# Summing all eight conditioning panels on TensorE, a new order of the first RWKV products, and a place of its own for the third RWKV weight panel

## The reference

```python
c_act = silu(c)
ada = c_act @ ada_w + ada_b                       # (1024) x (1024, 6144)
shift1, scale1, gate1, shift2, scale2, gate2 = split(ada, 6)
h = rms_norm(x, norm_mix_w) * (1 + scale1) + shift1
u = h @ w_in
da_q, da_k, da_v, hg_f, hg_i, hg_q, hg_g, rw_u, gates = split(u)
o_a, o_b, o_c = diff_attention(...), hgrn2(...), rwkv7(rw_u, ...)
x = x + gate1 * (the three branches, gated, projected and merged)
h = rms_norm(x, norm_ffn_w) * (1 + scale2) + shift2
x = x + gate2 * swiglu(h)
out = rms_norm(x, final_norm_w)
# in rwkv7: u = u + (u_prev - u) * mu, u_prev being u one token earlier
```

## Time and profile before

| what | us |
|---|---|
| median of 3 runs (1193.88 to 1200.45) | 1193.95 |
| the profiled execution | 1193.82 |
| its span | 1192.0 |
| PE busy in the span | 1106.1 |
| DVE busy | 622.2 |
| ACT busy | 469.2 |

### The profile page before, as it was taken

How to read it: one execution, slowest core, us unless ns; L and a number is a source line. 1 busy time by engine, 2 the same in 40 slices (tenths; PEclk the granted TensorE clock), 3 DMA queues, 4 the chain that set the end, 5 groups by cost and what they waited for, 6 DMA issues and landing times.

```text
span 1192.0 us, 18345 instructions
## 1 busy us (share of the span) xinstructions
PE 1106.1 (93%) x7721; PEld 895.2 (75%) x7721; DVE 622.2 (52%) x858; ACT 469.2 (39%) x576; POOL 28.0 (2%) x49
## 2 busy tenths in 40 slices
PE   3999999889999998889998999998999999999995
PEld 2788757778887677778776777877888888878874
DVE  4487665364453256865855549744255343243244
ACT  6332542323232446665646665254222222223222
POOL 0100000000000000002000010000000000000000
PEclk9999989999999999999999999998999999999997
DMA  9767413311012531119521167412344422322301
GB/s 343 264 208 247 153 62 125 102 47 46 12 47 82 210 115 62 54 54 294 193 96 45 62 242 253 168 54 71 106 142 140 141 93 85 106 102 75 106 1 71
DMA packets 106202, 145.44 MB, mean 122 GB/s; under 512 B 3188, under 2 KB 86376, under 8 KB 106120
## 3 DMA queue, kind: packets, MB, share of 16 engines
q1 hardware_dynamic: 92392, 107.15, 27.2%
q0 software_dynamic: 6240, 23.48, 5.7%
q10 hardware_dynamic: 7488, 13.63, 3.1%
HBM read 128.53 MB, written 15.73 MB: 121 GB/s over the span
## 4 chain that ended last, share of the span: by engine, by line
PE 73%; DVE 12%; ACT 9%; issue 3%; DMA 2%; ACTq 0%; SPq 0%; POOL 0%; DVEq 0%
PE bank L2019 72%; DVE wlo L1340 2%; ACT whi L859 1%; DMA qk<-early_out 1%; DMA cond<-in_ada_w 1%; ACT gate_row L874 1%; ACT LX L1027 1%; DVE x L1340 1%; DVE Z L1340 1%; DVE SC L1340 0%; DVE mg L1340 0%; DVE f_tmp L1340 0%; DVE q_lev L1340 0%; DVE y L1343 0%; ACT L1261 0%
## 5 line engine op out<-in xcount | busy, mean ns | idle before, releaser
L2019 PE MATMUL bank<-hhi,whi 128*128 128x512 f32 (+1 forms) x832 | 336.4, 404 | 14.2 <-DVE hlo L1340 7.4
L2019 PE MATMUL bank<-hlo,whi 128*128 128x512 f32 (+1 forms) x832 | 326.2, 392 | 0.0
L2019 PE MATMUL bank<-hhi,wlo 128*128 128x512 f32 (+1 forms) x832 | 325.6, 391 | 0.0
L1340 DVE TENSOR_TENSOR wlo<-raw,whi 128x2048 fp32r<-128x2048 f32 (+1 forms) x80 | 170.6, 2132 | 262.5 <-ACT whi L859 261.6
L859 ACT ACTIVATE whi<-raw 128x2048 fp32r<-128x2048 f32 (+1 forms) x80 | 143.0, 1788 | 225.3 <-PE bank L2019 194.2
L2019 PEld LDWEIGHTS bank<-hhi,whi 128*128 128x128 f32 x832 | 160.4, 193 | 57.0 <-DVE hlo L1340 8.4
L2019 PEld LDWEIGHTS bank<-hhi,wlo 128*128 128x128 f32 x832 | 159.9, 192 | 33.5
L2019 PEld LDWEIGHTS bank<-hlo,whi 128*128 128x128 f32 x832 | 160.4, 193 | 30.7 <-issue 0.5
L2019 PE MATMUL bank<-whi,d_hi 128*128 128x512 f32 x160 | 63.3, 396 | 3.3 <-DVE d_lo L1340 3.3
L2019 PE MATMUL bank<-wlo,d_hi 128*128 128x512 f32 x160 | 63.1, 395 | 0.0
L2019 PE MATMUL bank<-whi,d_lo 128*128 128x512 f32 x160 | 63.1, 395 | 0.0
(11 more groups left out here) (343 smaller groups left out, 1555.1 us busy)
## 6 DMA issues: line engine op xcount, KB each, us to landing
raw<-in_w_in SPq DMA_DIRECT2D x33, 1024.0 KB, 5.4
raw<-in_f_in SPq DMA_DIRECT2D x22, 1024.0 KB, 5.0
raw<-in_ada_w SPq DMA_DIRECT2D x16, 1024.0 KB, 5.3
early_out<-gate_row ACTq DMA_DIRECT2D x52, 256.0 KB, 2.1
raw<-in_f_out SPq DMA_DIRECT2D x11, 1024.0 KB, 4.8
cond<-in_ada_w SPq DMA_DIRECT2D x8, 1024.0 KB, 10.8
sg<-early_out POOLq DMA_DIRECT2D x4, 1536.0 KB, 11.5
raw<-in_w_out SPq DMA_DIRECT2D x4, 1024.0 KB, 5.1
```

The lines of the kernel that those rows point to most:

```text
L1340: return v.tensor_tensor(out_, a, b, op)
L2019: return t.matmul(out_, lhsT, rhs, start=start, stop=stop, skip_group_check=True)
```

## The change

- The sums of all eight "first" panels are made on PE by one function (`row(f)` in place of `scale(q)`); ACT copies each result into its place of `ada_acc`. DVE's four `ada_sum` calls and `s_shift_sum` go. A shift section now takes 2 matmuls in `ada`, as a scale section did.
- DVE writes `x_norm`, not ACT.
- w2 (m = 2) gets a place of its own (`third_hi`, `third_lo`, where cond 4 and cond 5 lay), and is split in the head: by ACT ahead of `first_h(6)`, by DVE after `first_low(7)`. In the loop each of ACT and DVE is then one weight panel further on: step n takes panel m = n + 2 where it took m = n + 1, with the late sums behind that panel; step 1 first makes the sums behind w2.
- PE's hand-written order of the first products is another.

Cut to its core (declarations of semaphores left out, `at`, slot lists and the second norm's count too):

```diff
@@ panel_slots
-    slots = [2 if m == total - spare else 3 if m == total - 1 else (m + (m > total - spare)) % RING for m in range(total)]
+    own = {2: RING + 2, total - spare: RING, total - 1: RING + 1}
+    shared = [m for m in range(total) if m not in own]
+    slots = [own[m] if m in own else shared.index(m) % RING for m in range(total)]
@@ bank_plan
     for q in range(4):
-        b.add("scale", q)
+        b.add("row", 2 * q)
+        b.add("row", 2 * q + 1)
@@ build
+        third_hi = at("third_hi", 80, [P, 2048], F32R)
+        third_lo = at("third_lo", 88, [P, 2048], F32R)
@@ cond_released
-            if f % 2:
-                eng.wait_ge(*full("scale", f // 2))
-            else:
-                eng.wait_ge(s_shift_sum, f // 2 + 1)
+            eng.wait_ge(*full("row", f))
@@ gpsimd
-            pool.wait_ge(s_shift_sum, 4)
-            pool.wait_ge(*full("scale", 3))
+            pool.wait_ge(*full("row", 7))
@@ scalar
-            def scale_row(q):
+            def row(f):
+                act.wait_ge(*full("row", f))
+                if f >= 2:
+                    act.wait_ge(*full("ada", ADA[f - 2]))
+                do(ada_acc[:, f % 2, 0, :], bank_of("row", f)[:, 0:256], ACT.Copy).then_inc(free_sem("row", f), 1)
+                act.wait_ge(*freed("row", f))
...
-            for tb in range(TB):
-                norm_scaled(0, tb, x_in, x_norm)
-            scale_row(0)
+            row(0)
+            row(1)
             split_hi()
             first_h(0)
             first_h(1)
-            scale_row(1)
+            row(2)
+            row(3)
             split_hi()
             first_h(2)
             first_h(3)
-            for q in range(2, 4):
-                scale_row(q)
-                first_h(2 * q)
-                first_h(2 * q + 1)
+            row(4)
+            row(5)
+            first_h(4)
+            first_h(5)
+            row(6)
+            row(7)
+            split_hi()
+            first_h(6)
+            first_h(7)
 
             for n in range(7):
-                if n:
+                if 0 < n < 6:
                     split_hi()
@@ vector
+            def sums_behind(i):
                 while i + 1 < len(panels) and panels[i + 1][0] == "ada":
                     i += 1
                     late_sum(i)
+            def take_panel():
+                m = split_next[0]
+                if m < len(weights):
+                    take_low()
+                    sums_behind(weights[m])
...
             for tb in range(TB):
                 row_rstd(0, tb)
-            ada_sum(0, first_at[0])
+                ts(x_norm[:, tb, :], x_in[:, tb, :], col(RSTD + tb), ALU.mult).then_inc(s_x_normed, 1)
+                dve.wait_ge(s_x_normed, up(s_x_normed))
             conditioned(0)
             take_panel()
...
-            ada_sum(1, first_at[2])
             conditioned(1)
             take_panel()
...
-            ada_sum(2, first_at[4])
             conditioned(2)
-            ada_sum(3, first_at[6])
             first_low(4)
             first_low(5)
             conditioned(3)
...
             first_low(6)
             first_low(7)
+            take_low()
 
             for n in range(7):
-                if n:
+                if n == 1:
+                    sums_behind(weights[2])
+                if 0 < n < 6:
                     take_panel()
@@ tensor
             def ada(n):
-                if n < 4:
-                    pe.wait_ge(s_shift_sum, n + 1)
-                elif n < 8:
-                    pe.wait_ge(*freed("scale", n - 4))
+                if n < 8:
+                    pe.wait_ge(*freed("row", ADA.index(n)))
...
-                parts = 1 if 4 <= n < 8 else 2
+                parts = 1 if n < 8 else 2
...
-            scale(0)
+            row(0)
+            row(1)
             ada(0)
             ada(4)
             transposes((0, 1))
-            scale(1)
+            units = [[begin("rw", 2 * n + m) for m in range(2)] for n in range(2)]
+            row(2)
+            row(3)
             transposes((2, 3))
             ada(1)
             ada(5)
-            units = [[begin("rw", 2 * n + m) for m in range(2)] for n in range(2)]
             first = [next_panel()]
             unit_part(first[0], 0, units[0], (0, 1))
+            row(4)
             first.append(next_panel())
             unit_part(first[1], 1, units[1], (0, 1))
-            unit_part(first[0], 0, units[0], (2, 3))
-            scale(2)
+            row(5)
             transposes((4, 5))
             ada(2)
             ada(6)
+            unit_part(first[0], 0, units[0], (2, 3))
             unit_part(first[1], 1, units[1], (2, 3))
-            scale(3)
+            row(6)
+            row(7)
             transposes((6, 7))
             ada(3)
+            ada(7)
             unit_part(first[0], 0, units[0], (4, 5))
-            ada(7)
+            unit_part(first[1], 1, units[1], (4, 5))
             unit_part(first[0], 0, units[0], (6, 7))
-            unit_part(first[1], 1, units[1], (4, 5))
             unit_part(first[1], 1, units[1], (6, 7))
```

More of the change, by code:

```diff
@@ L516, in build @@
         s_cond_in = [sem(f"cond_in{f}") for f in range(8)]
-        s_shift_sum = sem("shift_sum")
         s_ca_wide = sem("ca_wide")
@@ L570, in build @@
         s_normed = sem("normed")
+        s_x_normed = sem("x_normed")
         s_panel_hi = sem("panel_hi")
@@ L640, in build @@
         last_hi, last_lo = (tile[:, 0:4, :].rearrange("p k t -> p (k t)") for tile in (hhi, hlo))
-        hi_slots = [whi[:, 0, :], whi[:, 1, :], spare_hi[:, :], last_hi]
-        lo_slots = [wlo[:, 0, :], wlo[:, 1, :], spare_lo[:, :], last_lo]
+        hi_slots = [whi[:, 0, :], whi[:, 1, :], spare_hi[:, :], last_hi, third_hi[:, :]]
+        lo_slots = [wlo[:, 0, :], wlo[:, 1, :], spare_lo[:, :], last_lo, third_lo[:, :]]
         first_at = [i for i, (kind, _) in enumerate(panels) if kind == "first"]
@@ L1365, in ada_sum @@
                         dve.wait_ge(s_ada_step, step)
-                        done = s_shift_sum if n < 4 else s_panel_taken
-                        stt(acc, src[:, k, :], ca[:, k:k + 1], acc, ALU.mult, ALU.add).then_inc(done, 1)
-                        dve.wait_ge(done, up(done))
+                        stt(acc, src[:, k, :], ca[:, k:k + 1], acc, ALU.mult, ALU.add).then_inc(s_panel_taken, 1)
+                        dve.wait_ge(s_panel_taken, up(s_panel_taken))
             def ada_out(n):
@@ L1382, in ada_out, with take_low @@
                     dve.wait_ge(*freed("ada", n))
-            def take_panel():
+            def take_low():
                 m = split_next[0]
                 split_next[0] += 1
-                if m >= len(weights):
-                    return
                 i = weights[m]
@@ L2090, in transposes @@
             def transposes(kcs):
-                pe.wait_ge(s_normed, TB)
+                pe.wait_ge(s_x_normed, TB)
                 for kc in kcs:
@@ L2098, in second_transposes @@
             def second_transposes(q, kcs):
-                pe.wait_ge(s_normed, TB + 2 * q + 2)
+                pe.wait_ge(s_normed, 2 * q + 2)
                 for kc in kcs:
@@ L2133, in _, with row @@
             pe.wait_ge(s_ca_wide, 1)
-            def scale(q):
-                src = loaded(pe, first_at[2 * q + 1]).rearrange("p (k n) -> p k n", k=KC)
-                ps = begin("scale", q)
+            def row(f):
+                src = loaded(pe, first_at[f]).rearrange("p (k n) -> p k n", k=KC)
+                ps = begin("row", f)
                 for k in range(KC):
@@ L2141, in scale @@
                     last = mm(ps[rows, 0:256], ca_wide[:, k, :], src[:, k, :], k < 4, k >= KC - 4)
-                end(last, "scale", q)
+                end(last, "row", f)
             def unit_part(slot, n, tiles, kcs):
```

## The result

The changed kernel takes 1211.84 us (median of 4 runs, 1211.44 to 1216.01), the kernel before 1194.39 us in the same comparison: a ratio of 1.0138, 95% interval 1.0102 to 1.0173. The forecast was 1214.9 us, with a range of 1207 to 1222. The profiled execution has a span of 1210.0 us, 18.0 above that of before.

What follows compares the result with a forecast made beforehand. The prediction took PE, busy 93% of the span, to bound the kernel. From 1193.82 us it took 4.6 for the head and added 19.4 for waits and 6.3 for clock: 1214.9 us, range 1207 to 1222.

Steps and rivals of the forecast that it cites:

- The three waits: Loop, before n = 4, 5 and 6: PE waits for DVE's late bank read-out, 6.46 us each, 19.4 us in all.
- rival (b): Loop: slow stretches lose 3.2 us each (1218.2 us), or a fourth wait is added (1223.5 us); chance 0.08.
- The clock behind the waits: Loop, products after the three PE waits: half-clock stretches lose 2.1 us each, 6.3 us in all.
- rival (a): Loop: the waits come with little or no loss of clock, 1208.6 us; chance 0.10.
- The loop as a whole: Loop, n = 4 to 6: PE waits of 19.4 us plus clock loss of 6.3 us, 25.7 us.
- The head: Before n = 2: gain of 4.6 us, with n = 2 starting at 62.35 for 66.94.
- The wait for `hlo`: Head, PE at 54.36 waiting for block 6: goes through the new order, gain 2.8 us.
- the 2.8 + 1.7 of the prediction: Head: 2.8 us from the vanished wait for `hlo`, 1.7 us from the half-clock stretch that followed it.
- the slow start stays (4.84 us): Head, first 12 product matmuls: still slow at 4.84 us, possibly 3.4 to 5.2 by phase.
- `x_norm` on DVE: Head: taken as 0.9 us, bounds 0.51 and 1.17, hidden by the transposes at either end.
- Rival (d): Head: the 2.79 us wait stays, as ACT is kept by the split of w2, 1219.4 us; chance 0.05.
- Rival (c): Loop: rw 4's bank is read out in time, so no wait, 1189.2 us; chance 0.07.

Runs made afterwards that it cites:

- experiment 1: Changed kernel with DVE's two read-outs moved ahead of the late sums in each loop step: 1186.94 us, ratio 0.9936 to the kernel before.
- experiment 3: Changed kernel, DVE's order kept, with four places for the late sums instead of two: 1187.1 us, ratio 0.9942 to the kernel before.
- Experiment 4: Kernel before with only the loop of ACT and DVE moved on by one panel: 1217.0 us, ratio 1.0189.
- Experiment 5: Changed kernel with 52 unused matmuls behind the late sections of n = 3 and of n = 4, filling two PE waits: 1207.75 us.
- experiments 6: Kernel of experiment 1 with the first products in the order of the kernel before: 1191.45 us, ratio 0.9978 to the kernel before.
- 12: Kernel of experiment 2 with shift panels summed by DVE and `x_norm` by ACT, so no row sums: 1190.99 us, ratio 0.9965 to the kernel before.
- experiment 8: Kernel of experiment 1 with `x_norm` written by ACT as in the kernel before: 1184.15 us, ratio 0.992 to the kernel before.
- experiment 1 again: Kernel of experiment 1 unchanged, run once more as parent in a later comparison: 1187.45 us.
- the held kernel of experiments 9 to 11: Kernel of experiment 1 with PE waiting for cond 3 ahead of row 2, not behind it: 1187.58 us, its parent 1187.45 us.
- experiment 2: Changed kernel with the loop of ACT and DVE at its old lag, third panel still split in the head: 1189.4 us, ratio 0.9957 to the kernel before.
- experiment 7: Kernel of experiment 2 with w2 back in the ring of two and split in the loop: 1191.64 us, ratio 0.9976 to the kernel before.

## Why the prediction was right

**The three waits** were forecast at 6.46 us each, before n = 4, 5 and 6, and measured at 6.45, 6.45 and 6.44. The count (three, not at n = 3, none behind n = 6) held too; rival (b), a fourth wait or stretches that lose 3.2 us each, did not occur. Experiments 1 and 3 show both links of the argument separately: take either the read-out from behind the sum, or the sum from behind PE, and all is gone. Experiment 4 shows that nothing else of the change takes part.

**The clock behind the waits** was forecast at 3 x 2.1 = 6.3 us and measured at 2.7 + 2.0 + 1.6 = 6.3. Experiment 5 shows it to be the clock's. The sizes repeat: experiment 4 lost 2.7, 2.1 and 1.6 us in the same three products, and experiment 5 lost 2.2 behind the wait left empty. That the sum came out to a tenth is partly luck all the same, since the 2.1 a wait was a choice between bounds of 1.2 and 3.2. The rule weighed there (the Trainium skill, "TensorE: Matmul & The Clock Gate", Loop structure matters more than you think: idle time between bursts makes the next burst run throttled) agrees with all three waits of this trace (granted 0.79, 0.84 and 0.86 in the product behind them), and rival (a) falls. The loop as a whole: 25.7 forecast, 25.9 measured.

**The head** is the term that was mis-sized: 4.6 us forecast, 8.2 measured at the start of n = 2. The wait for `hlo` went, as forecast (experiments 6 and 12); the third panel's product follows without a gap; the order and the third place alone give 66.9 - 62.4 = 4.5 us, which is the 2.8 + 1.7 of the prediction. What failed is the step "the slow start stays (4.84 us)". In the changed kernel the 12 first matmuls take 2.92 us, from 28.82 to 31.74, and the 8 section records 1.06 instead of 1.73 us. (The prediction gave the kernel before 4.84 us for its first 12; that window ends where the 12th starts, and they took until 36.63, 5.17 us.) The start gained 31.46 - 28.82 = 2.6 us for the 1.5 forecast, and the slow stretch behind it about 2.2 more. With the 1.1 us at the start this makes 3.3 us more than forecast, against the 3.6 by which the head came out better and the 3.1 us by which the time did. The 3.6 us are those of one execution: the profiles with the same order and the third place reached n = 2 between 56.79 (experiment 8) and 60.73 (experiment 1 again), all of them with row sums and all ahead of the 62.35 forecast; without row sums (experiment 12) it was 62.44.

All eleven profiles with row sums have the full clock by the end of the first dozen matmuls, ten of them from the first one on; the three without (before, experiments 4 and 12) have it some 5 us after the first. That much is shown, for profiles. What it is in the row sums is not: PE is busier ahead of the products, but the held kernel of experiments 9 to 11, with 2.60 us of idle time there for 0.74 in its parent, had the clock in time. So the cause of the earlier rise stays open.

**`x_norm` on DVE** took 0.75 us a block for the 0.9 taken, and is hidden at either end (experiment 8). Rival (d), ACT kept by the split of w2, is refuted by the same profile: ACT split w2 from 46.56 to 48.47, and PE has no wait between the first product and the one ahead of n = 4. Rival (c), a read-out in time, did not occur.

## What to carry to other kernels

Moving an engine's loop one item ahead moves everything of that item, also the waits. Before an item is taken earlier, list for each instruction what it waits for and what stands behind it in program order; here two places for partial sums tied DVE to PE, and the bank's read-out was queued behind that tie. The slack (6.3 us) against the shift (one step, 12.7 us) gave each wait to 0.02 us before a run. And a busy share tells nothing on this: DVE was at 51%, and PE waited for it. The mend was to put what frees a resource ahead of what may wait.

## What the runs showed that I had not expected

The spread of one kernel's runs (1184.3 to 1191.5 in experiment 1, in 10 runs) is as large as most parts of the head, so parts of 1 to 2 us can be read from a profile's timeline but not confirmed by a median. A part of the spread goes with the clock elsewhere: in experiment 8 the fastest run (1181.23) had a granted clock of 0.982 over the whole execution and the slowest (1190.52) one of 0.975. The profiled execution of experiment 8 has no slow stretch between its head and 155 us, that of experiment 1 has one from about 135 (0.73 from 135 to 140).

DVE's split of the third panel took 2.85 us in the changed kernel, where the same instruction takes 2.29 on the ring's places. The timelines of GpSimd and DVE, first in the changed kernel, then in experiment 2, put it beside GpSimd's only cast:

```profile
52.04 0.92 POOL L782 CAST lev<-lev_f 128x832 uint8<-128x832 f32 x1 [2.32 <-DMA lev_f<-in_levels]
52.26 2.85 DVE L1346 TENSOR_TENSOR third_lo<-raw,third_hi 128x2048 fp32r<-128x2048 f32 x1
```

```profile
51.56 2.29 DVE L1346 TENSOR_TENSOR third_lo<-raw,third_hi 128x2048 fp32r<-128x2048 f32 x1
...
51.79 2.80 POOL L782 CAST lev<-lev_f 128x832 uint8<-128x832 f32 x1 [2.77 <-DMA lev_f<-in_levels]
```

Whichever of the two starts second is the one that takes longer: DVE by 0.56 us, GpSimd by 1.9, as if one had to wait for the other to finish. The same holds in experiments 1, 8 and 12 (the cast first, 2.85 us). It was hidden here.

An idle time of PE ahead of a burst is not enough to foretell its clock: 2.53 us of wait in experiment 7 were followed by a stretch that began at full clock and fell to half within the burst, 1 us after its start. And 1.73 us were enough in the head of experiment 2: its transposes at 18.33 ran at full clock (8 records in 1.07 us), and the row behind the wait, at 21.13, took 1.93 us, which is half clock. The timeline of PE in experiment 7; the spacing from start to start goes from 0.23 to 0.42 us:

```profile
61.31 0.50 PE L2029 MATMUL bank<-hhi,whi 128*128 128x512 f32 x1 [2.53 <-DVE wlo L1345]
61.65 0.40 PE L2029 MATMUL bank<-hlo,whi 128*128 128x512 f32 x1
61.88 0.39 PE L2029 MATMUL bank<-hhi,wlo 128*128 128x512 f32 x1
...
62.38 0.63 PE L2029 MATMUL bank<-hlo,whi 128*128 128x512 f32 x1
62.80 0.63 PE L2029 MATMUL bank<-hhi,wlo 128*128 128x512 f32 x1
```
